# A hybrid encoder step: the exponentials of the prompt heads are turned undivided, and six bits of a search stand between row maxima

## The chip, the core and the metric

The kernel runs on one core of one Trainium2 chip. The metric is the time of one execution in device microseconds. A core has five engines that work side by side and wait for one another by semaphores: TensorE (PE, matmuls; PEld is its weight load), VectorE (DVE), ScalarE (ACT), GpSimd (POOL) and SyncE (SP, which issues DMAs). Each engine works through its own instructions strictly in the order in which the code issues them; a wait stops everything behind it on that engine.

## The reference

One step of a trunk with two layers, on a prompt of 512 tokens and on 8 samples of 16 new tokens with 1024 cached ones. Layer 0 mixes the tokens by sparse attention: an indexer scores the keys, each query keeps its best k, and softmax attention with 8 heads runs over them. Cut to that part (the rest, a gated MLP in layer 1, a convolutional feed-forward and a gated addition in both, is not touched by the change):

```python
s = einsum('bqhd,bkd->bqhk', qi, ki) * (IDX_DIM ** -0.5)
score = einsum('bqhk,bqh->bqk', relu(s), wi * (N_IDX_HEADS ** -0.5))
score = where(admissible, score, NEG_INF)
_, idx = lax.top_k(score, k_sel)          # 128 for the prompt, 256 for a sample
logits = einsum('bqgrd,bqkgd->bqgrk', qg, kg) * (HEAD_DIM ** -0.5)
p = softmax(where(valid, logits, NEG_INF), axis=-1)
o = einsum('bqgrk,bqkgd->bqgrd', p, vg)   # then o @ w_out
```

## The kernel before, in words

All 640 token columns (512 of the prompt, 128 of the samples) go through together, in tiles of 128. Every product with weights is done in three float32r passes (high x high, high x low, low x high), so ScalarE splits off the high part of each block of weights and VectorE the low part. Nothing is scheduled by a tool: the order on each engine is the order of the Python code of that engine's block, and the semaphores are written out by hand.

The selection masks the keys instead of gathering them. For the samples, the 256th largest score of each of 128 rows (8 samples x 16 tokens) is found by a search over its bits from 30 down to 0. One bit (`search`) is three VectorE instructions: a comparison of the 1040 scores with a guess, which also counts, and two on a single column that set the next guess. The table `BITS` says how many bits are done during which tile of the projections (tiles 4 to 8: 5, 6, 6, 6 and 8). `hide_samples` makes of the last guess the mask `bias_s`, with a scan that settles ties. For the prompt, rounds of `find` (the 8 largest of a row) and `mark` (strike them out) select the keys; the rounds left over stand between the row maxima of the samples and of the stage p1.

Attention is a list `att` of 40 heads, numbered s: 0 to 7 are the heads of the first prompt tile (stage p0, 128 keys), 8 to 15 the samples (all 8 heads of a sample are one entry, 1040 keys), 16 to 23, 24 to 31 and 32 to 39 the heads of prompt tiles 1 to 3 (p1, p2 and p3, with 256, 384 and 512 keys). All engines first wait in `after_projection`. Then each runs its own loop over s:

- TensorE, in turn s: `turn_probs(s-1)` transposes the probabilities into PSUM, `weigh(s-2)` multiplies them with the values, `turn_rows(s-3)` (for samples alone) turns the result, `scores(s+1)` makes mask plus logits of the next head.
- VectorE: `row_max(s)` takes the reciprocal of the sum of head s-1, then the negated maximum of head s.
- ScalarE, in turn s: `normalise(s-1)` divides the exponentials of a prompt head, then comes the exponential of s with its sum, `turn_out_probs(s-1)` (the transposed probabilities out of PSUM), `take_turned(s-3)` for samples, `take_out(s-2)` (the result out of PSUM).

For a prompt head the probabilities are divided before they are transposed, and the weighting has the values as the stationary operand, so its result comes out turned already. For a sample the raw exponentials are transposed, the result is divided as it leaves PSUM (into `o_row`), turned by TensorE, and copied into `qT`.

Before turn NA-3 (s = 37), the first block of the output projection's weights is split: `split_hi` on ScalarE, `split_lo` on VectorE. Behind the last head ScalarE casts the results (`a_hi`, L986), VectorE subtracts (`a_lo`, L1297), and the output projection starts (L638).

## Time and profile before

| | |
|---|---|
| median of 3 runs | 1687.17 us (1685.6 to 1688.04) |
| profiled execution, its own time | 1686.9 us |
| its span | 1685.0 us |
| TensorE busy | 1615.4 us (96%), 11098 matmuls |
| VectorE busy | 928.8 us (55%) |
| ScalarE busy | 629.7 us (37%) |
| mean granted TensorE clock | 0.985 of full |
| chain that ended last | PE 87%, DVE 7%, ACT 3%, issue 2% |

The span goes from the first to the last instruction in the trace; the time of an execution is a little longer. A busy share is a mean over stages that have different limits, and matmuls are pipelined with modelled ends, so a busy TensorE need not be one at its peak. The chain is followed back from the last instruction, at each step to what released it.

### The profile page before, as it was taken

The page shows a single profiled execution, that of the slowest core. Times are in us where ns is not written, and L with a number is a line of the kernel's source. Part 1 is how long each engine was busy: PE and PEld are TensorE (multiplying, and loading weights), DVE is VectorE, ACT ScalarE, POOL GpSimd, SP SyncE. Part 2 cuts the span into 40 slices and gives each one's busy share as a digit, 9 for nine tenths or more (in the row PEclk, how much of TensorE's full clock was granted, in tenths as well). Part 3 has the DMA queues.
Part 4 walks back from the last instruction along what each step waited for, and adds up shares of the span by engine and source line. Part 5 has one row for each costly group of instructions (what it writes and reads, how often), then busy time and mean ns, then how long its engine had stood idle before and what let it go on. Part 6 is the DMA issues. An engine that isn't in the chain of part 4 may idle for free.

```text
span 1685.0 us, 25745 instructions
## 1 busy us (share of the span) xinstructions
PE 1615.4 (96%) x11098; PEld 1544.5 (92%) x11106; DVE 928.8 (55%) x1287; ACT 629.7 (37%) x928; POOL 172.1 (10%) x270
## 2 busy tenths in 40 slices
PE   7999778889999999999999999999999999999998
PEld 7759745589999999999999999999999999999998
DVE  5279966344665256525665715527663466346653
ACT  4546444744332133213354524325331233123441
POOL 2000000002110011001121201022110011001200
PEclk9999889999999999999999999999999999999999
DMA  5212445021122212221132221321222122211321
GB/s 216 80 50 76 161 167 200 1 76 68 59 76 101 74 53 76 95 71 61 67 110 84 88 85 52 115 75 51 75 76 101 51 75 75 100 51 63 113 92 47
DMA packets 27938, 143.50 MB, mean 85 GB/s; under 512 B 3393, under 2 KB 7105, under 8 KB 14641
## 3 DMA queue, kind: packets, MB, share of 16 engines
q1 hardware_dynamic: 26912, 139.03, 23.5%
q0 software_dynamic: 768, 2.81, 0.5%
q8 instruction: 87, 1.43, 0.4%
q14 instruction: 27, 0.21, 0.0%
q10 hardware_dynamic: 144, 0.02, 0.0%
HBM read 136.29 MB, written 5.43 MB: 84 GB/s over the span
## 4 chain that ended last, share of the span: by engine, by line
PE 87%; DVE 7%; ACT 3%; issue 2%; DMA 0%; SPq 0%; DVEq 0%; ACTq 0%
PE psum L638 71%; PE psum L684 5%; DVE bias_s L1202 2%; PE psum L724 2%; PE psum L552 1%; PE psum L491 1%; PE psum L500 1%; PE psum L594 1%; DVE stat L1248 1%; PE psum L673 1%; PE psum L539 1%; DVE w_lo L1291 1%; PE psum L587 1%; PE psum L511 1%; PE psum L569 1%
## 5 line engine op out<-in xcount | busy, mean ns | idle before, releaser
L638 PE MATMUL psum<-a_hi,w_hi 128*128 128x384 f32 (+2 forms) x1920 | 439.2, 310 | 7.5 <-DVE a_lo L1297 7.5
L638 PE MATMUL psum<-a_lo,w_hi 128*128 128x384 f32 (+2 forms) x1920 | 437.8, 309 | 0.0
L638 PE MATMUL psum<-a_hi,w_lo 128*128 128x384 f32 (+2 forms) x1920 | 437.7, 309 | 0.0
L638 PEld LDWEIGHTS psum<-a_hi,w_hi 128*128 128x128 f32 x1920 | 341.7, 188 | 9.7 <-issue 6.7
L638 PEld LDWEIGHTS psum<-a_hi,w_lo 128*128 128x128 f32 x1920 | 342.3, 188 | 0.0
L638 PEld LDWEIGHTS psum<-a_lo,w_hi 128*128 128x128 f32 x1920 | 342.2, 188 | 0.0
L1291 DVE TENSOR_TENSOR w_lo<-w_raw,w_hi 128x2048 fp32r<-128x2048 f32 (+1 forms) x101 | 227.2, 2250 | 120.7 <-ACT w_hi L983 120.6
L983 ACT ACTIVATE w_hi<-w_raw 128x2048 fp32r<-128x2048 f32 (+1 forms) x102 | 189.6, 1859 | 172.1 <-PE psum L638 172.1
L638 PE MATMUL psum<-g_hi,w_hi 128*128 128x320 f32 x832 | 191.0, 311 | 2.4 <-DVE u_act L1503 1.6
L1139 ACT ACTIVATE conv<-conv_in,convw 128x656 f32<-128x656 f32 x88 | 82.4, 937 | 293.5 <-DVE conv_in L1537 293.5
L638 PE MATMUL psum<-g_hi,w_lo 128*128 128x320 f32 x832 | 189.9, 310 | 0.0
L638 PE MATMUL psum<-g_lo,w_hi 128*128 128x320 f32 x832 | 189.9, 310 | 0.0
L1474 DVE TENSOR_TENSOR xT<-psum,xT 128x640 f32<-128x640 f32 x64 | 52.7, 823 | 197.7 <-PE psum L638 197.3
L1536 DVE TENSOR_TENSOR conv_in<-psum,inv_rms 128x512 f32<-128x512 f32 x88 | 60.6, 688 | 153.4 <-PE psum L638 153.3
L638 PEld LDWEIGHTS psum<-g_hi,w_hi 128*128 128x128 f32 x832 | 139.4, 189 | 4.0 <-issue 2.2
L638 PEld LDWEIGHTS psum<-g_hi,w_lo 128*128 128x128 f32 x832 | 139.7, 189 | 0.0
L638 PEld LDWEIGHTS psum<-g_lo,w_hi 128*128 128x128 f32 x832 | 139.7, 189 | 0.0
L1597 POOL COPY tails<-conv_in 128x18 f32<-128x18 f32 x88 | 44.1, 501 | 661.3 <-DVE conv_in L1537 661.3
L684 PE MATMUL psum<-w_hi,a_hi 128*128 128x256 f32 x288 | 83.1, 289 | 0.0
L684 PE MATMUL psum<-w_lo,a_hi 128*128 128x256 f32 x288 | 82.4, 286 | 0.0
L684 PE MATMUL psum<-w_hi,a_lo 128*128 128x256 f32 x288 | 82.3, 286 | 0.0
L1544 DVE SCALAR_TENSOR_TENSOR conv<-conv_in,convw,conv 128x656 f32<-128x656 f32 x88 | 79.4, 902 | 3.1
(228 smaller groups left out, 1944.1 us busy)
## 6 DMA issues: line engine op xcount, KB each, us to landing
w_raw<-in_weights SPq DMA_DIRECT2D x93, 1024.0 KB, 4.8
key_b<-in_keyT SPq DMA_DIRECT2D x8, 1024.0 KB, 7.9
val_b<-in_val SPq DMA_DIRECT2D x8, 1024.0 KB, 4.8
w_raw<-in_weights SPq DMA_DIRECT2D x8, 768.0 KB, 4.1
kidx_b<-in_kidxT SPq DMA_DIRECT2D x8, 512.0 KB, 3.5
xT<-in_xT SPq DMA_DIRECT2D x2, 1280.0 KB, 6.8
out_yT<-xT SPq DMA_DIRECT2D x8, 320.0 KB, 2.2
xT<-in_xT SPq DMA_DIRECT2D x3, 640.0 KB, 8.4
```

The costliest lines, as they stand in the source:

```text
L491: pe.matmul(psum[:, c, 0:w], qi_blk[:, b, :], kidx_b[b % 2][:, k0:k0 + w], start=True, stop=True).then_inc(idx_ready, 1)
L638: last = pe.matmul(psum[:, 2 * j + bank, 0:t1 - t0], w[:, k, P * j:P * j + P], x[:, k, t0:t1], start=(k == 0 and n == 0), stop=(k == K - 1 ...
L684: last = pe.matmul(out, x[:, k, P * t:P * t + P], ww[:, k, :], start=(k == 0 and n == 0), stop=(k == KC - 1 and n == 2))
L724: last = pe.matmul(psum[:, 2 * (c % 2) + i, 0:T // 2], w[:, k, P * c:P * c + P], x[:, k, i * T // 2:(i + 1) * T // 2], start=(k == 0 and n ...
L983: act.activation(w_hi(u)[:, 0:n], w_raw[u % 2][:, 0:n], ACT.Copy).then_inc(w_hi_ready, 1)
L1139: act.activation(co[j][:, :], ci[j][:, 2:2 + CW], ACT.Identity, bias=convw[:, l, ch, 3:4], scale=convw[:, l, ch, 2:3])\
L1202: dve.tensor_scalar(bias_s[:, :], score_s[:, :], f32(guess[:, 0:1]), 0.0, ALU.is_ge, ALU.add, accum_out=found[:, 1:2]).then_inc(counted, 1)
L1291: dve.tensor_tensor(w_lo(u)[:, 0:n], w_raw[u % 2][:, 0:n], f32(w_hi(u)[:, 0:n]), ALU.subtract)\
L1474: dve.tensor_tensor(xn, bank2(j, T // 2), xn, ALU.add).then_inc(free_dve, 1)
L1536: dve.tensor_tensor(halves(ci[j][:, 2:2 + TP]), bank2(j, 256), halves(inv_rms[:, 0:TP]), ALU.mult)
L1544: dve.scalar_tensor_tensor(out=co[j][:, :], in0=ci[j][:, 0:CW], scalar=convw[:, l, ch, 0:1], in1=co[j][:, :], op0=ALU.mult, op1=ALU.add).t ...
L1597: ins = pool.tensor_copy(tails[:, j * FC + c, :].rearrange("p (i e) -> p i e", e=2), padded(conv_in[c % 2][j], NB + 1))
```

## The change

Two parts. First, the exponentials of a prompt head are no longer divided on ScalarE (`normalise` and its semaphore are gone): TensorE transposes them raw, the weighting takes them as the stationary operand and the values as the moving one, and then prompt heads go the way of the samples: `take_out` scales by the inverse sum into `o_row`, `turn_rows` turns that on TensorE, `take_turned` copies it into `qT`. Second, tile 8 of the projections holds two bits of the search in place of eight; the last six stand one each between the row maxima 0 to 6 of p0, and `hide_samples` comes behind them in one piece, with row maximum 7 after it.

```diff
--- before.py
+++ after.py
@@ -49,7 +49,8 @@
 TOPK_P, TOPK_S = 128, 256
 KV = 3
 WIDE_ROUNDS = 10
-BITS = {4: 5, 5: 6, 6: 6, 7: 6, 8: 8}
+BITS = {4: 5, 5: 6, 6: 6, 7: 6, 8: 2}
+LATE_BITS = 6
 ZQ, ZK, ZV, ZQI, ZKI, ZW, ZEND = 0, 1024, 1280, 1536, 2048, 2112, 2120
 PADW = 2 + TP + NB * (2 + TQ) + 16
 CW = TP + NB * (2 + TQ)
@@ -306,19 +307,17 @@
         att += [("p", j, h) for j in range(1, 4) for h in range(H)]
         NA = len(att)
         S0, S1 = H, H + NB
-        att_p = [s for s in range(NA) if att[s][0] == "p"]
         bias_ready, n_bias_ready = sem("bias_ready"), counts(["p0", "s", "p1", "p2", "p3"])
         logits, n_logits = sem("logits"), counts(range(NA))
         neg_max, n_neg_max = sem("neg_max"), counts(range(NA))
         exp_done, n_exp_done = sem("exp_done"), counts(range(NA))
         sum_inverse, n_sum_inverse = sem("sum_inverse"), counts(range(NA))
-        prob_ready, n_prob_ready = sem("prob_ready"), counts(att_p)
         pt_ready, n_pt_ready = sem("pt_ready"), counts(range(NA))
         pt_taken, n_pt_taken = sem("pt_taken"), counts(range(NA))
         out_ready, n_out_ready = sem("out_ready"), counts(range(NA))
         out_taken, n_out_taken = sem("out_taken"), counts(range(NA))
-        o_scaled, n_o_scaled = sem("o_scaled"), counts(range(S0, S1))
-        o_turned, n_o_turned = sem("o_turned"), counts(range(S0, S1))
+        o_scaled, n_o_scaled = sem("o_scaled"), counts(range(NA))
+        o_turned, n_o_turned = sem("o_turned"), counts(range(NA))
         s_key = [sem(f"s_key{i}") for i in range(KV)]
         s_val = [sem(f"s_val{i}") for i in range(KV)]
         key_new, n_key_new = sem("key_new"), counts(range(NB))
@@ -556,10 +555,7 @@
 
             def turn_probs(s):
                 kind, a, h = att[s]
-                if kind == "p":
-                    pe.wait_ge(prob_ready, n_prob_ready[s])
-                else:
-                    pe.wait_ge(exp_done, n_exp_done[s])
+                pe.wait_ge(exp_done, n_exp_done[s])
                 if kind == "p":
                     if S1 <= s < S1 + 3:
                         pe.wait_ge(pt_taken, n_pt_taken[S1 - 1])
@@ -584,8 +580,8 @@
                 o = psum[:, 6 + s % 2, :]
                 if kind == "p":
                     for i in range(a + 1):
-                        last = pe.matmul(o[:, 0:P], vtok[:, i, P * (h // R):P * (h // R) + P],
-                                         probsT[s % 2][:, i, :], start=(i == 0), stop=(i == a))
+                        last = pe.matmul(o[:, 0:P], probsT[s % 2][:, i, :],
+                                         vtok[:, i, P * (h // R):P * (h // R) + P], start=(i == 0), stop=(i == a))
                 else:
                     pe.wait_ge(s_val[a % KV], 32 * (a // KV + 1))
                     for i in range(9):
@@ -606,7 +602,7 @@
                     turn_probs(s - 1)
                 if 2 <= s < NA + 2:
                     weigh(s - 2)
-                if S0 <= s - 3 < S1:
+                if s >= 3:
                     turn_rows(s - 3)
                 if s + 1 < NA:
                     scores(s + 1)
@@ -881,30 +877,21 @@
                 kind, a, h = att[s]
                 act.wait_ge(out_ready, n_out_ready[s])
                 o = psum[:, 6 + s % 2, 0:P]
+                act.wait_ge(sum_inverse, n_sum_inverse[s])
+                act.activation(o_row[s % 2][:, :], o, ACT.Copy, scale=stat[:, 3, s:s + 1]).then_inc(o_scaled, 1)
+
+            def take_turned(s):
+
+                kind, a, h = att[s]
+                act.wait_ge(o_turned, n_o_turned[s])
+                o = psum[:, 6 + s % 2, P:2 * P]
                 if kind == "p":
                     act.activation(qT[:, h, P * a:P * a + P], o, ACT.Copy).then_inc(out_taken, 1)
                 else:
-                    act.wait_ge(sum_inverse, n_sum_inverse[s])
-                    act.activation(o_row[s % 2][:, :], o, ACT.Copy, scale=stat[:, 3, s:s + 1]).then_inc(o_scaled, 1)
-
-            def take_turned(s):
-
-                kind, a, h = att[s]
-                act.wait_ge(o_turned, n_o_turned[s])
-                act.activation(qT[:, :, TP + TQ * a:TP + TQ * a + TQ],
-                               psum[:, 6 + s % 2, P:2 * P].rearrange("p (h q) -> p h q", q=TQ), ACT.Copy)\
-                   .then_inc(out_taken, 1)
-
-            def normalise(s):
-
-                kind, a, h = att[s]
-                pr = probs[s % 2][:, 0:P * (a + 1) if kind == "p" else KEYS]
-                act.wait_ge(sum_inverse, n_sum_inverse[s])
-                act.activation(pr, pr, ACT.Copy, scale=stat[:, 3, s:s + 1]).then_inc(prob_ready, 1)
+                    act.activation(qT[:, :, TP + TQ * a:TP + TQ * a + TQ], o.rearrange("p (h q) -> p h q", q=TQ), ACT.Copy)\
+                       .then_inc(out_taken, 1)
 
             for s in range(NA + 3):
-                if s - 1 in n_prob_ready:
-                    normalise(s - 1)
                 if s < NA:
                     kind, a, h = att[s]
                     w = P * (a + 1) if kind == "p" else KEYS
@@ -918,7 +905,7 @@
                     split_hi(FIRST["attn_out"])
                 if 1 <= s <= NA:
                     turn_out_probs(s - 1)
-                if S0 <= s - 3 < S1:
+                if s >= 3:
                     take_turned(s - 3)
                 if 2 <= s < NA + 2:
                     take_out(s - 2)
@@ -1217,15 +1204,11 @@
                 dve.tensor_scalar(found_eq[:, :], score_s[:, :], last, None, ALU.is_equal)
                 link(dve.tensor_scalar(bias_s[:, :], score_s[:, :], last, 0.0, ALU.is_gt, ALU.add,
                                        accum_out=found[:, 2:3]))
-                row_max(1)
                 dve.tensor_tensor_scan(found_rank[:, :], found_eq[:, :], found_eq[:, :], 0.0, ALU.add, ALU.bypass)
                 link(dve.tensor_scalar(found[:, 3:4], found[:, 2:3], -1.0, float(TOPK_S), ALU.mult, ALU.add))
-                row_max(2)
                 link(dve.scalar_tensor_tensor(out=found_eq[:, :], in0=found_rank[:, :], scalar=found[:, 3:4],
                                               in1=found_eq[:, :], op0=ALU.is_le, op1=ALU.mult))
-                row_max(3)
                 link(dve.tensor_tensor(found_eq[:, :], found_eq[:, :], bias_s[:, :], ALU.add))
-                row_max(4)
                 dve.tensor_scalar(bias_s[:, :], found_eq[:, :], 0.5, NEG, ALU.is_lt, ALU.mult).then_inc(bias_ready, 1)
 
             def hide(j):
@@ -1251,8 +1234,11 @@
             link(dve.memset(bias_p[0][:, :], 0.0))
             dve.memset(bias_p[0][0:64, 64:P], NEG).then_inc(bias_ready, 1)
             row_max(0)
+            for bit in range(LATE_BITS - 1, -1, -1):
+                search(dve, link, [bit])
+                row_max(LATE_BITS - bit)
             hide_samples()
-            for s in range(5, S0):
+            for s in range(LATE_BITS + 1, S0):
                 row_max(s)
             for s in range(S0, S1):
                 row_max(s)
```

On VectorE, at the start of attention, before: the last bits of the search, the first mask of p0, row maximum 0, and then `hide_samples` with the next row maxima in it.

```order
L1202 TENSOR_SCALAR bias_s,found<-score_s,guess 128x1040 [waits dve_chain]
L1205 TENSOR_SCALAR guess<-found 128x1 [waits counted]
L1210 TENSOR_TENSOR guess<-guess 128x1 [waits dve_chain]
L1251 MEMSET bias_p0 128x64 [waits turned_out,s_kout,free_act,dve_chain]
L1252 MEMSET bias_p0 64x64 [waits dve_chain]
L1248 TENSOR_REDUCE stat<-psum 128x1 [waits logits]
L1217 TENSOR_SCALAR found_eq<-score_s,guess 128x1040
L1218 TENSOR_SCALAR bias_s,found<-score_s,guess 128x1040
L1239 RECIPROCAL stat<-stat 128x1 [waits exp_done,dve_chain]
L1248 TENSOR_REDUCE stat<-psum 128x1 [waits logits]
L1221 SCALAR_TENSOR_TENSOR found_rank<-found_eq 128x1040
```

In the changed kernel the first mask stands behind the second bit of tile 8, and bits follow on row maxima.

```order
L1189 TENSOR_SCALAR bias_s,found<-score_s,guess 128x1040 [waits dve_chain]
L1192 TENSOR_SCALAR guess<-found 128x1 [waits counted]
L1194 SCALAR_TENSOR_TENSOR guess<-guess 128x1 [waits dve_chain]
L1234 MEMSET bias_p0 128x64 [waits turned_out,s_kout,free_act,dve_chain]
L1235 MEMSET bias_p0 64x64 [waits dve_chain]
L1231 TENSOR_REDUCE stat<-psum 128x1 [waits logits]
L1189 TENSOR_SCALAR bias_s,found<-score_s,guess 128x1040
L1192 TENSOR_SCALAR guess<-found 128x1 [waits counted]
L1194 SCALAR_TENSOR_TENSOR guess<-guess 128x1 [waits dve_chain]
L1222 RECIPROCAL stat<-stat 128x1 [waits exp_done,dve_chain]
L1231 TENSOR_REDUCE stat<-psum 128x1 [waits logits]
L1189 TENSOR_SCALAR bias_s,found<-score_s,guess 128x1040
```

The six bits moved behind the first mask and row maximum 0; the reciprocals and maxima stay one each per head.

On TensorE, one turn of stage p2, before: transposes, weighting, mask, logits (`probs0` and `probs1` are the two buffers of the exponentials).

```order
L569 MATMUL psum<-ident,probs0 128x128 [waits pt_taken,prob_ready]
L569 MATMUL psum<-ident,probs0 128x128 x2
L587 MATMUL psum<-probsT1,vtok 128x128 [waits out_taken,pt_taken]
L587 MATMUL psum<-probsT1,vtok 128x128 x2
L538 MATMUL psum<-bias_p2,ident_b 128x384 [waits exp_done]
L539 MATMUL psum<-kT,qT 128x384
```

The same turn in the changed kernel.

```order
L565 MATMUL psum<-ident,probs0 128x128 [waits pt_taken,exp_done]
L565 MATMUL psum<-ident,probs0 128x128 x2
L583 MATMUL psum<-vtok,probsT1 128x128 [waits out_taken,pt_taken]
L583 MATMUL psum<-vtok,probsT1 128x128 x2
L597 MATMUL psum<-ident,o_row0 128x128 [waits o_scaled]
L537 MATMUL psum<-bias_p2,ident_b 128x384 [waits exp_done]
L538 MATMUL psum<-kT,qT 128x384
```

The transposes wait for the exponential itself, the two operands of the weighting have changed sides, and one transpose of `o_row` stands ahead of the mask and the logits of the next head.

On ScalarE, one turn of p2 and the start of the next, before.

```order
L915 ACTIVATE probs1,stat<-psum,stat 128x384 [waits pt_ready,neg_max]
L874 ACTIVATE probsT0<-psum 128x384 [waits out_ready,pt_ready]
L885 ACTIVATE qT<-psum 128x128 [waits out_ready]
L903 ACTIVATE probs1<-probs1,stat 128x384 [waits sum_inverse]
L915 ACTIVATE probs0,stat<-psum,stat 128x384 [waits pt_ready,neg_max]
```

The same in the changed kernel.

```order
L902 ACTIVATE probs1,stat<-psum,stat 128x384 [waits pt_ready,neg_max]
L870 ACTIVATE probsT0<-psum 128x384 [waits out_ready,pt_ready]
L889 ACTIVATE qT<-psum 128x128 [waits o_turned]
L881 ACTIVATE o_row1<-psum,stat 128x128 [waits sum_inverse,out_ready]
L902 ACTIVATE probs0,stat<-psum,stat 128x384 [waits pt_ready,neg_max]
```

The 384 columns wide division is gone, and of the two instructions of 128 columns one waits for the turned row and one for the inverse sum.

## Rows read from the trace of the kernel before

**Rows 1.** The page's chain that ended last: shares of the span by line.
```profile
PE psum L638 71%; PE psum L684 5%; DVE bias_s L1202 2%; PE psum L724 2%; PE psum L552 1%; PE psum L491 1%; PE psum L500 1%; PE psum L594 1%; DVE stat L1248 1%; PE psum L673 1%; PE psum L539 1%; DVE w_lo L1291 1%; PE psum L587 1%; PE psum L511 1%; PE psum L569 1%
```

**Rows 2.** Timeline, VectorE, p0: start, length, engine, line, out<-in, count [idle before<-releaser].
```profile
201.81 1.29 DVE L1202 TENSOR_SCALAR_CACHE_REDUCE bias_s<-score_s,guess 128x1040 bf16<-128x1040 f32 x1
...
203.53 1.30 DVE L1202 TENSOR_SCALAR_CACHE_REDUCE bias_s<-score_s,guess 128x1040 bf16<-128x1040 f32 x1
...
205.29 0.11 DVE L1251 MEMSET bias_p<- 128x64 uint32 x1
...
206.78 0.75 DVE L1217 TENSOR_SCALAR found_eq<-score_s,guess 128x1040 f32<-128x1040 f32 x1
...
213.71 0.29 DVE L1248 TENSOR_REDUCE stat<-psum 128x1 f32<-128x128 f32 x1 [0.48 <-PE psum L539]
...
216.16 0.16 DVE L1239 RECIPROCAL stat<-stat 128x1 f32<-128x1 f32 x1
...
220.54 0.29 DVE L1248 TENSOR_REDUCE stat<-psum 128x1 f32<-128x128 f32 x1 [0.58 <-PE psum L539]
```

**Rows 3.** Timeline, ScalarE and the sync queue (SPq), end of the projections.
```profile
195.97 1.30 ACT L1090 ACTIVATE kT<-psum 128x640 f32<-128x640 f32 x2
...
197.33 0.69 SPq L436 DMA_DIRECT2D key_b<-in_keyT  x1
```

**Rows 4.** Groups by line, 197 to 350: count | busy us, mean ns | idle before<-releasers.
```profile
L903 ACT ACTIVATE probs<-probs,stat 128x128 f32<-128x128 f32 (+3 forms) x32 | 17.9, 560 | 4.9 <-DVE stat L1239 4.7
...
L569 PE MATMUL psum<-ident,probs 128*128 128x128 f32 x80 | 16.7, 307 | 16.2 <-ACT probs L903 15.8
```

**Rows 5.** Stretches: us, busy PE, PEld, DVE, ACT, POOL, PE clock, DMA share, GB/s.
```profile
197.00:206.00 9.00, 0.27 (x2) 0.30 (x3) 7.95 (x22) 0.26 (x1) 0.98 (x4) 0.59 0.94 347
...
222.00:224.00 2.00, 2.00 (x9) 0.50 (x9) 0.00 (x0) 0.02 (x1) 0.00 (x0) 0.88 0.00 0
...
335.00:340.00 5.00, 1.86 (x11) 0.99 (x9) 2.73 (x3) 3.22 (x6) 0.00 (x0) 1.00 0.00 0
```

**Rows 6.** Timeline, TensorE, score matmuls of samples 0 and 4.
```profile
223.51 1.08 PE L552 MATMUL psum<-key_b,q_smp 128*64 128x512 f32 x4
...
251.30 1.98 PE L552 MATMUL psum<-key_b,q_smp 128*64 128x512 f32 x4
```

**Rows 7.** Timeline, TensorE, in p1 (first row) and p2.
```profile
287.53 0.44 PE L569 MATMUL psum<-ident,probs 128*128 128x128 f32 x2 [0.48 <-ACT probs L903]
...
314.03 0.55 PE L569 MATMUL psum<-ident,probs 128*128 128x128 f32 x3 [0.32 <-ACT probs L903]
314.41 0.83 PE L587 MATMUL psum<-probsT,vtok 128*128 128x128 f32 x6
...
315.24 0.81 PE L539 MATMUL psum<-kT,qT 128*128 128x384 f32 x2
316.12 0.55 PE L569 MATMUL psum<-ident,probs 128*128 128x128 f32 x3
```

**Rows 8.** Timeline, VectorE, p1 to p3: row maxima, and the split of weights.
```profile
293.08 0.42 DVE L1248 TENSOR_REDUCE stat<-psum 128x1 f32<-128x256 f32 x1
...
295.14 0.42 DVE L1248 TENSOR_REDUCE stat<-psum 128x1 f32<-128x256 f32 x1
...
301.23 0.42 DVE L1248 TENSOR_REDUCE stat<-psum 128x1 f32<-128x256 f32 x1 [0.79 <-PE psum L539]
...
303.14 0.56 DVE L1248 TENSOR_REDUCE stat<-psum 128x1 f32<-128x384 f32 x1 [0.69 <-PE psum L539]
...
320.78 0.69 DVE L1248 TENSOR_REDUCE stat<-psum 128x1 f32<-128x512 f32 x1 [1.14 <-PE psum L539]
...
333.94 0.69 DVE L1248 TENSOR_REDUCE stat<-psum 128x1 f32<-128x512 f32 x1 [0.82 <-PE psum L539]
337.27 2.29 DVE L1291 TENSOR_TENSOR w_lo<-w_raw,w_hi 128x2048 fp32r<-128x2048 f32 x1 [2.64 <-ACT w_hi L983]
```

**Rows 9.** Timeline, ScalarE, the cast of the output projection's operand.
```profile
348.77 5.13 ACT L986 ACTIVATE a_hi<-qT 128x640 fp32r<-128x640 f32 x8
```

## The prediction

> **What bounds the kernel now.** I read the chain of waits on the page first: 71% of the span is one line, the TensorE products of L638, and the search bits (DVE, L1202), the sample scores (L552) and the row maxima (L1248) hold 1 to 2% each [rows 1]. So the products outside attention cannot move by this change; what can move lies between the end of the projections (about 197 us) and the first product of the output projection (350 us). I then read the timelines of the engines in this stretch, one stage at a time, and asked in each which wait ends last.
>
> Stage p0 (heads 0 to 7) cannot begin before the VectorE has done eight search bits: it writes the first mask at 205.29 [rows 2], though the last projected tile is there at 197.27 and the sync queue, which waits for the same three semaphores, goes on at 197.33 [rows 3]. The samples follow; they wait for one another's exponentials and for their keys. In p1 (heads 16 to 23) the VectorE sets the pace, with a round of find and mark per head (2.06 us from one row maximum to the next). In p2 and p3 it is TensorE together with the division on ScalarE: TensorE stood idle 15.8 us in all before its transposes, released by L903 [rows 4].
>
> **Part one: six bits moved into p0.** A bit takes 1.72 us (201.81 to 203.53) [rows 2]. Eight of them back from 205.29 begin near 191.5; two would be done by 195, so the VectorE then starts p0 with the sync queue at 197.33. From the first mask to the end of the first row maximum it took 205.29 to 206.78, 1.49, so row maximum 0 is done at 198.8. Then come six rounds of a bit and a row maximum. The maximum costs some 0.3 (0.29 by its row, the reciprocal before it overlaps), so 2.02 a round, 12.1 together; I add 0.25 because the first reciprocal waits for the first exponential and its table load. TensorE and ScalarE have 2 us for each head there and took 1.71 before (four heads from 213.71 to 220.54), so they don't hold the VectorE up: 211.2. Hiding the samples took 206.78 to 216.16, with four row maxima and a wait of 0.48 inside: 9.38 - 4 x 0.3 - 0.48 = 7.7, now in one piece, and row maximum 7 is behind it. It starts near 219.0, before at 220.54 [rows 2]: 1.5 earlier. The VectorE thus starts 8 us earlier, carries 10.3 us more, and loses its idle gaps.
>
> What is late next is TensorE's clock. In the second half of p0 it had work close together, and the granted clock came back in 222:224 (0.88 of full), just as sample 0 began. In the change TensorE has nothing from about 213 to 219.5, while the samples are hidden. After its idle stretch in 197:206 the clock had fallen (0.59 in the mean) [rows 5]. A group of four score matmuls took 1.98 us at half clock and 1.08 at full [rows 6]; sample 0 has two and its masks, so all at half clock it costs up to 1.8 more than at full, and part of it was at half before. Ends: 1.5 saved, the clock as before; or 0.3 lost, sample 0 all at half. I take half of the way: **-0.7**.
>
> The Trainium skill (TensorE: Matmul & The Clock Gate, section "HAM oscillation") says that a gap between bursts of matmuls can put the array back to half rate, so that the next burst starts cold. By that rule this part would be +0.3 and the whole sum -4.1. The trace agrees in 197:206, but not everywhere: in 335:340 TensorE was busy 1.86 of 5.00 us and kept 1.00 [rows 5]; by that row it is -1.5 and the sum -5.9.
>
> The samples themselves keep their order. Three more turned rows (heads 5 to 7) fall into their first steps, where TensorE waits for an exponential anyway; without that cover they cost 0.13 each.
>
> **Part two: the division leaves the path.** Removed: 32 divisions of the exponentials on ScalarE, 0.56 each in the mean [rows 4], and the wait of the transposes for them, which also held a VectorE reciprocal. Added per prompt head: one TensorE transpose and a ScalarE copy from PSUM. Three transposes hold TensorE 0.38 (314.03 to 314.41) [rows 7], so one is 0.13. The copy that goes out of PSUM was there already; now there are two small ones for one small and one wide. The new waits: the turned row stands in TensorE's queue ahead of the next head's scores and waits for the scaled row; ScalarE's copy of it stands ahead of the next scaled row. Both look back one whole head, so in a head of 2 us they are met early. The operands of the weighting change sides, at the same 128x128.
>
> - p1. The pace of find and mark stays (293.08 to 295.14) [rows 8]. What goes is the waits ahead of it and behind it. TensorE waited 0.48 for the division of head 16 [rows 7], and as long for that of 17; without the first, the scores of head 18 are 0.6 earlier, and VectorE runs its rounds 0.6 earlier. Behind the last round VectorE waited 0.79 for head 23's scores (301.23), and head 24's came at 303.14 [rows 8]; both chains lose a division with its handover, about 1.0 together. Ends: nothing (VectorE alone bounds), -2.2. I take **-1.6**.
> - p2. Now 303.14 to 320.78 for eight heads, 2.205 each [rows 8]. TensorE's own work is at most 2.09 (transposes at 314.03 and 316.12); the second start came just after a division's end, so there is a wait in it. It begins the weighting 0.17 before the modelled end of the transposes; if it can do so behind the product at 315.24 (0.81), its own work is 1.85 [rows 7]. With 0.13 for the turned row: 1.98 to 2.22. I take 2.05, as TensorE stood idle in every second head: 8 x 0.155 = **-1.2** (ends -1.8 and +0.1).
> - p3. Five intervals from 320.78 to 333.94, 2.63 each [rows 8]; transposes, weighting and product grow with the width, and the same reasoning leaves 0.08 a head: **-0.4** (ends -1.0 and +0.5).
> - Tail. The split of the next weights (2.29 on VectorE at 337.27) [rows 8] stays, between heads 37 and 38, and the first operand is cast at 348.77 [rows 9]. From the split's end (339.56) that is 9.2 us with two divisions of 512 columns on the path; each costs its time, a reciprocal and two handovers, about 1.0. Against that the last head has a turned row and one more copy behind it, 0.8. Ends 0 and -2; I take **-1.2**.
>
> Sum: -0.7 - 1.6 - 1.2 - 0.4 - 1.2 = -5.1. From there on TensorE has work without a gap, so the shift reaches the end whole. The profiled execution had a span of 1685.0 in a time of 1686.9; it gives 1681.8. It lay 0.3 under the median of the runs, 1687.17, which gives 1682.1. I forecast 1682.0 us, 0.3% faster.
>
> **Rivals.**
> First: TensorE is already the bound in p2 and p3, so that each added transpose is paid there. For it: 2.09 of own work in 2.205 [rows 7, 8]. Against it: the 15.8 us idle before the transposes. Then p2 and p3 lose 16 x 0.13 - 0.1 = 2.0 in place of gaining 1.6: -5.1 + 3.6 = -1.5, 1685.7.
> Second: the clock takes p0's gain and falls again in the tail, where TensorE has shorter bursts; the output projection would then start at half clock for some us, like the sample that took 1.98 for 1.08 [rows 6], about 2 us lost. For it: the fall after 197. Against it: 335:340 at 1.00 [rows 5]. -5.1 + 1.0 + 2 = -2.1, 1685.1.
> Third, slower: the way of the result closes a ring: weighting, scaled row, turned row, copy, and the weighting two heads on waits for the copy. If it is longer than two heads, TensorE stands at the turned row as long as it stood at the division, and the 24 later heads pay 0.13 and, say, one more handover of 0.1: +5.5, with the tail's 0.8 and no gain in p0: +6.3, 1693.5. It decides only if scaled row, turn and copy with their handovers, some 1.3 us, take over 3; I see no row for that.
> Fourth: the moved bits do nothing, since VectorE is the engine that p0 waits for in both: part one 0, 1682.8. That is within the forecast's range.
>
> **How the numbers follow.** Forecast with the fourth 0.72, first 0.12, second 0.11, third 0.05. A difference of 0.2%, 3.4 us, is about what a measurement here tells from none; 1683.8 is the border. The forecast's cases go from -8 (1679; all the lower ends would be -8.5) to -3 (1684), with a tenth of them beyond the border. So faster 0.72 x 0.9 + 0.23 x 0.3 = 0.72, slower 0.05 and a little of the others, 0.06, the same 0.22. The range goes from 1678.6 to 1685.9, which takes in the first two rivals' values.
>
> **What would show it.** In the profile after: the first row maximum near 198.5 and the last of p0 near 219; a clock of 0.5 at the start of sample 0; no wait of the transposes for a division; p2 at 2.05 a head; the operand cast near 343.7. I am wrong if TensorE waits for the scaled rows, if p2 stays at 2.2, or if the samples take longer than before between row maximum 7 and the first of p1.

## The result, and the profile after

The changed kernel takes 1679.66 us (median, 1676.94 to 1680.47), the kernel before, beside it on the same chip, 1687.61; the ratio is 0.9946, 95% interval 0.993 to 0.9962. The ratio makes 1678.1 of the median that I started from, 1687.17; I forecast 1682.0 with 1678.6 as the lower end. So the change gains 7.5 us by its median, 8.0 beside the runs of the same chip and 9.1 by the ratio, where I said 5.1. The profiled execution, at 1676.94, is the fastest of four: span 1675.0, 10.0 below that of before. The chain that ended last is now 92% TensorE, 3% VectorE and 2% ScalarE.

The p0 stage in the timeline of VectorE after (start, length, line, operation, [idle before <- releaser]): the first mask, row maxima 0, 7 and 8.

```profile
197.35 0.11 DVE L1234 MEMSET bias_p<- 128x64 uint32 x1 [2.61 <-ACT kT L1077]
...
198.32 0.29 DVE L1231 TENSOR_REDUCE stat<-psum 128x1 f32<-128x128 f32 x1 [0.68 <-PE psum L538]
...
218.76 0.27 DVE L1231 TENSOR_REDUCE stat<-psum 128x1 f32<-128x128 f32 x1
224.04 1.24 DVE L1231 TENSOR_REDUCE stat<-psum 128x1 f32<-128x1040 f32 x1 [4.32 <-PE psum L551]
```

Row maximum 7 is 1.78 earlier than in [rows 2] (I said 1.5), but that of sample 0 only 0.94 earlier. TensorE shows why, at the samples' start:

```profile
219.58 0.61 PE L548 MATMUL psum<-bias_s,onehot 128*128 128x512 bf16 x1 [6.49 <-ACT probs L902]
220.12 1.98 PE L551 MATMUL psum<-key_b,q_smp 128*64 128x512 f32 x4
```

It idled 6.49 us behind head 6, and the first score group takes 1.98: half clock. Before, the same group took 1.34; the 1.08 at 223.51 in [rows 6] is the second group, which takes 1.09 now.

```profile
221.91 1.34 PE L552 MATMUL psum<-key_b,q_smp 128*64 128x512 f32 x4 [0.49 <-ACT probsT L874]
```

The granted clock was at half long ahead of the pause, and in both kernels: 0.50 in every slice of 4 us from 206 to 222. So the pause didn't bring it down. Before, it came back within this first group; now sample 0 starts 1.8 us earlier, and it comes back behind it.

The p2 stage on TensorE, one head from the transposes to the next head's, answers to [rows 7]:

```profile
304.76 0.49 PE L565 MATMUL psum<-ident,probs 128*128 128x128 f32 x3
305.09 0.83 PE L583 MATMUL psum<-vtok,probsT 128*128 128x128 f32 x6
305.76 0.27 PE L597 MATMUL psum<-ident,o_row 128*128 128x128 f32 x1
305.87 0.33 PE L537 MATMUL psum<-bias_p,ident_b 128*128 128x384 bf16 x1
306.03 0.81 PE L538 MATMUL psum<-kT,qT 128*128 128x384 f32 x2
306.67 0.49 PE L565 MATMUL psum<-ident,probs 128*128 128x128 f32 x3
```

No row has a wait, and each begins before the modelled end of the one ahead. From start to start: transposes 0.33, weighting 0.67, turned row 0.11, bias 0.16, scores 0.64, together 1.91. The lines from 197 to 340 us (count | busy, mean ns | idle before <- releasers) answer to [rows 4]:

```profile
L565 PE MATMUL psum<-ident,probs 128*128 128x128 f32 x80 | 15.4, 291 | 4.1 <-ACT probs L902 3.9
...
L597 PE MATMUL psum<-ident,o_row 128*128 128x128 f32 x40 | 12.2, 304 | 0.6 <-ACT o_row L881 0.6
```

The idle time before the transposes has gone from 16.2 to 4.1 us, and the turned rows wait 0.6 in all, for 40 of them: the ring of the third rival is nowhere closed.

The table holds the stretches of every profile, from start to start of row maxima (by the timeline of VectorE; s is the index of the attention step) and, for the tail, to the cast of the output operand. "Mark" is the start of an earlier, unchanged split of weights, ahead of attention; the column behind it is the way from there to sample 0.

| kernel | mark | mark to s=8 | samples 8-16 | p1 16-24 | p2 24-32 | p3 32-37 | tail | cast at |
|---|---|---|---|---|---|---|---|---|
| before | 127.63 | 97.35 | 58.06 | 20.10 | 17.64 | 13.16 | 14.83 | 348.77 |
| after | 127.47 | 96.57 | 55.39 | 18.21 | 15.24 | 12.01 | 13.84 | 338.73 |
| after_again | 127.70 | 96.56 | 56.10 | 19.84 | 15.24 | 12.01 | 13.84 | 341.29 |
| bits_only | 126.17 | 98.27 | 57.40 | 21.71 | 17.67 | 13.16 | 17.17 | 351.55 |
| raw_only | 127.92 | 94.57 | 58.56 | 19.83 | 15.24 | 12.01 | 13.84 | 341.97 |
| turn_twice | 126.27 | 97.59 | 57.79 | 19.94 | 16.00 | 12.56 | 14.26 | 344.41 |
| spread_bits | 126.31 | 95.73 | 56.69 | 19.82 | 15.24 | 12.01 | 13.83 | 339.63 |
| bit3 | 127.84 | 96.06 | 57.10 | 19.83 | 15.24 | 12.01 | 13.84 | 341.92 |
| before_keys | 125.19 | 98.50 | 51.77 | 20.10 | 17.64 | 13.16 | 17.17 | 343.53 |
| raw_keys | 126.45 | 95.36 | 52.08 | 18.21 | 15.24 | 12.01 | 13.83 | 333.18 |
| keys_first | 125.12 | 97.50 | 52.13 | 18.21 | 15.24 | 12.01 | 13.84 | 334.05 |
| spread_keys | 125.13 | 95.36 | 51.06 | 19.19 | 15.24 | 12.01 | 13.83 | 331.82 |

From the cast to the end it is 1335.5 to 1338.0 us in all twelve (1336.2 before, 1336.3 after), so between these two the table holds the whole difference. p2, p3 and the tail are the same to 0.01 in all kernels with part two, except the one that doubles the turned row. p1 has two levels, 18.21 and 19.82 to 19.94 with part two (19.19 once), 20.10 and 21.71 without; the longer one goes with a granted clock of 0.59 to 0.99 in 278:286, the shorter with 1.00. The samples and the way to them vary. The way from the mark to sample 0 also hangs on where the mark lies: before and before_keys have the same code up to there and 97.35 and 98.50, after and keys_first 96.57 and 97.50, raw_only and raw_keys 94.57 and 95.36; the earlier mark has the longer way each time.

### The profile page after: what moved, and what is told of

It is laid out like the page before. It is cut to its first block, busy times and chain, and to the rows that moved or that the text cites. A ratio compares the mean times of both kernels' runs of the same rounds, so it can differ in the third digit from the quotient of the medians.

```text
span 1675.0 us, 25851 instructions
## 1 busy us (share of the span) xinstructions
PE 1617.9 (97%) x11138; PEld 1548.9 (92%) x11138; DVE 927.9 (55%) x1287; ACT 621.4 (37%) x928; POOL 168.1 (10%) x270
## 4 chain that ended last, share of the span: by engine, by line
PE 92%; DVE 3%; ACT 2%; issue 1%; DMA 0%; SPq 0%; ACTq 0%; DVEq 0%
PE psum L634 71%; PE psum L680 9%; PE psum L720 2%; PE psum L551 1%; PE psum L490 1%; PE psum L583 1%; PE psum L499 1%; PE psum L590 1%; PE psum L538 1%; PE psum L669 1%; PE psum L510 1%; PE psum L565 1%; ACT a_hi L973 1%; DMA xT<-in_xT 0%; PE psum L759 0%
```

## Experiments

Each median stands beside the median of before on the same chip: 1688.11 for the first four kernels, 1687.27 for the next four, 1687.68 for the last two.

**after_again.** The changed kernel once more, no edit.

> The changed kernel once more. Of the 10.0 us between the two profiled spans, 2.7 lie between row maximum 8 and row maximum 16, in the samples, which neither part of the change touches. Theory A: these 2.7 are TensorE's clock, which fell to half inside two samples of the profiled execution before and in none after, and that differs from one execution to the next; then a profile taken here can show half clock in a sample again, the samples are then as long as before, and the times lie some 7 to 9 us under the kernel before, spread over 3 us. Theory B: the change itself shortens the samples; then the samples are again 55.4 us from row maximum 8 to 16, and the clock stays full in them.

1680.4 us (1679.87 to 1682.82), ratio 0.9953 [0.9937, 0.997]. The granted clock fell to 0.72 and 0.86 in 262:266 and 266:270, and to 0.85 and 0.72 in 278:286, where the first profile had 1.00 throughout: p1 took 1.63 longer than in the first profile, the samples 0.71. That is theory A, though the samples are not as long as before (56.10 for 58.06). So the first profile is a lucky one: 10.0 is not what the change is worth in most executions.

**bits_only.** Part one without part two: the kernel before with the bits moved, divisions on the exponentials as they were.
```
-BITS = {4: 5, 5: 6, 6: 6, 7: 6, 8: 8}
+BITS = {4: 5, 5: 6, 6: 6, 7: 6, 8: 2}
+LATE_BITS = 6
...
+            for bit in range(LATE_BITS - 1, -1, -1):
+                search(dve, link, [bit])
+                row_max(LATE_BITS - bit)
             hide_samples()
```

> Part one alone: six bits between the row maxima of p0, the division stays. Theory A (the parts add up): sample 0's row maximum comes 0.9 us earlier than before, as in the changed kernel, the stages p1 to p3 keep the paces of before (2.2 us in p2, 2.6 in p3), and the time is about 1 us under before, 0.5 to 1.5. Rival: the bits need the short way of the raw exponentials, because TensorE and ScalarE with the division take longer per head than a bit and a row maximum (1.98 us); then row maximum 7 comes at or after 220.5 and the time is the same as before or up to 2 us longer.

1688.84 us, ratio 1.0003 [0.9991, 1.0015]: nothing, so the parts don't add up as theory A has it. The rival gave the right time for a reason that doesn't hold: row maximum 7 is not late (217.86, 91.69 behind the mark for 92.91 before). What it gains is lost between it and row maximum 8, 6.58 for 4.44: sample 0 runs at half clock (its two score groups take 1.98 and 1.91). Its profile also has a clock fall in the tail, after the split of the weights (TensorE there, same columns as above):

```profile
340.88 1.11 PE L570 MATMUL psum<-ident,probs 128*128 128x128 f32 x4 [3.59 <-ACT probs L904]
341.79 1.91 PE L588 MATMUL psum<-probsT,vtok 128*128 128x128 f32 x8
```

In the kernel before, the same place reads

```profile
340.44 0.66 PE L569 MATMUL psum<-ident,probs 128*128 128x128 f32 x4 [3.59 <-ACT probs L903]
...
340.94 1.06 PE L587 MATMUL psum<-probsT,vtok 128*128 128x128 f32 x8
```

The wait for the division is the same 3.59, yet the eight weighting products take 1.91 for 1.06, and the tail 17.17 for 14.83.

**raw_only.** Part two without part one.
```
-BITS = {4: 5, 5: 6, 6: 6, 7: 6, 8: 2}     # and LATE_BITS = 6 between the row maxima
+BITS = {4: 5, 5: 6, 6: 6, 7: 6, 8: 8}     # row maxima 1 to 4 inside the samples' mask, as before
```

> Part two alone: raw exponentials are turned and the sum divides the result; all eight bits in tile 8, the samples hidden between row maxima as before. Theory A: p1 to the cast of the output projection's operand gains what the profile of the changed kernel shows there, 1.9 + 2.4 + 1.2 + 1.0 = 6.5 us, p0 up to 1 more, since its last heads have no division either; the time is 6.5 to 7.5 us under before. Rival: half of the gain is the early start and its changed clock, so that this one is only 4 us or less under before.

1676.74 us (1675.43 to 1680.33), ratio 0.9931 [0.9914, 0.9948]: the whole gain, if not more (its interval overlaps those of the changed kernel). It is also more than theory A said, 11.4 by the median and 8.8 at the least by the interval: p0 gives 2.8 (97.35 to 94.57), not up to 1. Row maximum 7 is as early as with part one (218.53), and TensorE reaches sample 0 in work and at full clock:

```profile
218.91 0.27 PE L596 MATMUL psum<-ident,o_row 128*128 128x128 f32 x1
219.69 1.08 PE L550 MATMUL psum<-key_b,q_smp 128*64 128x512 f32 x4 [0.50 <-ACT probsT L869]
```

From the mark to sample 0 it is 94.57, 2.0 less than with both parts.

**turn_twice.** The changed kernel with every prompt head's row turned a second time.
```
+                    pe.transpose(psum[:, 6 + s % 2, P:2 * P], o_row[s % 2][:, :], ident[:, :])
```

> The changed kernel with every prompt head's result turned twice by TensorE (the second transposes the same row into the same place). Theory A: in p2 and p3 TensorE's own work is the pace (1.91 and 2.40 us), so each head of these 16 pays one more transpose, 0.11: p2 at 2.02, p3 at 2.51, 1.8 us in all and 0.2 in the tail, while p1, paced by VectorE at 1.91, pays nothing; 2 us over the changed kernel. Rival: the chain of maximum, exponential, copies and their handovers is the pace; then the second transpose hides and the time is that of the changed kernel within 0.5 us.

1683.4 us (1680.55 to 1685.52), ratio 0.9966 [0.9953, 0.9978]. p2 goes from 1.905 to 2.00 a head and p3 from 2.40 to 2.51: one turned row's 0.11 is paid (almost) whole in both. In p2 and p3 TensorE's own work is the pace now; in p1 it is not (19.94 beside 19.84 in after_again, both with the fall of the clock). The median is 3.0 over after_again where 2 was expected; p2, p3 and the tail of the profile hold 1.7 of it.

**spread_bits.** VectorE's work of the first tile dealt out differently.
```
-            for bit in range(LATE_BITS - 1, -1, -1):     # one bit, one row maximum; then the mask in one piece
+            for s in range(1, 4):                         # two bits, one row maximum;
+                search(dve, link, [2 * (3 - s) + 1])      # row maxima 4 to 7 between the mask's operations
+                search(dve, link, [2 * (3 - s)])
+                row_max(s)
```

> The changed kernel with the same VectorE work in the first tile, dealt out differently: two search bits ahead of each of row maxima 1 to 3, and row maxima 4 to 7 between the operations that make the samples' mask, so that no block of the mask's operations stands ahead of row maximum 7. Theory (part one's gain of row maximum 7 is given back because TensorE idles 6.49 us while VectorE makes the mask in one piece, and comes to sample 0 at half clock): row maximum 7 stays near 218.8 or comes a little earlier, the longest pause of TensorE in that stretch falls below 3 us, the granted clock at 218 to 222 is 1.00, row maximum 8 comes at 222.5 to 223.0 instead of 224.0, and the time is 1 to 1.5 us below the changed kernel. Rival (the order of VectorE's work is of no account, the samples wait for their mask in any case): row maximum 8 stays at 223.8 to 224.3 and the time within 0.5 us.

1678.17 us, ratio 0.9952 [0.9935, 0.9969]: 1.5 under the changed kernel by the medians, level with it by the ratios (0.9946 and 0.9953), so the times don't show the gain; mark to sample 0 is 95.73, 0.84 less than after. The pause of TensorE is 0.81 as the theory says, but the clock is not back:

```profile
217.85 1.98 PE L551 MATMUL psum<-key_b,q_smp 128*64 128x512 f32 x4 [0.81 <-ACT probsT L870]
```

So what the profile gains comes from row maximum 7 (216.35; 1.25 nearer to the mark than after's, since VectorE makes the mask no longer in one block), and the half clock doesn't need the long pause: it was 0.50 from 202 to 218, 0.64 in 218:222. That part of the theory fell. In raw_only TensorE was busy 3.90 of 4.00 us in 214:218, the clock rose there (0.74), and 218:222 had 1.00.

**raw_keys** and **keys_first.** SyncE's queue, with part two alone and with the whole change.
```
+            for b in range(NB):
+                if b <= KV:
+                    load_keys(b)
+                if KV <= b < NB - 1:
+                    load_keys(b + 1)
+                load_values(b)
```

`load_keys` and `load_values` hold the lines that stood in this loop; there, the keys of a sample stood behind the wait of the values of the sample ahead of it.

> Part two alone, with one more edit: SyncE issues the keys of sample b+1 ahead of the values of sample b, whose issue waits for a buffer of the values; before, the keys stood behind that wait. Theory (TensorE's waits ahead of a sample's scores, 1.62, 0.40, 1.04 and 1.14 us in the changed kernel's profile, are for keys that were issued late, and the stretches of half clock in the samples follow such waits): these waits fall below 0.3 us each, the samples take 53 us or less from row maximum 8 to 16 (55.4 in the changed kernel's profile, 56.3 and 58.6 in other profiles at a half clock in part of it), with granted clock 1.00 throughout; the time is 3 to 5 us below part two alone (1676.7), and the runs spread less. Rival (the transfers themselves are the limit, or the values wait in the keys' place): the wait moves to the values or the next keys, the samples take 55 us or more, and the time is within 1 us of part two alone.

> The changed kernel with the same edit of SyncE's order as raw_keys (keys of sample b+1 ahead of the values of sample b). Theory: as there, the waits for keys go and the samples take 53 us or less; the time is 3 to 5 us below the changed kernel (1679.7), and it stays 2 to 4 us above raw_keys, since part one adds a cold sample 0 and nothing more. Rival one (transfers are the limit): within 1 us of the changed kernel. Rival two (part one does help where the samples no longer wait): the time is equal to raw_keys or below it.

1671.37 us (1670.93 to 1673.14), ratio 0.9904 [0.9888, 0.9919], and 1671.66 (1670.81 to 1673.64), 0.9905 [0.9889, 0.9921]. The changed kernel waited before its sample scores for keys (one of four such rows; "issue" says that the profile names no releaser, and that it is the keys is shown by the edit):

```profile
247.16 0.38 PE L548 MATMUL psum<-bias_s,onehot 128*128 128x512 bf16 x1 [1.62 <-issue]
```

All four are gone from both, the samples take 52.1 and the clock is 1.00 in all of 234:286; the same stretch of raw_only (us, busy PE, PEld, DVE, ACT, POOL, PE clock, DMA share, GB/s) had

```profile
262.00:266.00 4.00, 2.35 (x7) 0.50 (x10) 1.29 (x6) 0.28 (x2) 0.00 (x0) 0.74 0.85 299
...
278.00:286.00 8.00, 5.89 (x51) 4.86 (x52) 3.99 (x14) 2.41 (x8) 0.00 (x0) 0.79 0.58 237
```

and keys_first

```profile
262.00:266.00 4.00, 3.85 (x49) 2.82 (x48) 3.90 (x11) 2.81 (x6) 0.00 (x0) 1.00 0.20 78
...
278.00:286.00 8.00, 7.77 (x71) 5.99 (x72) 6.05 (x18) 4.43 (x17) 0.00 (x0) 1.00 0.00 0
```

The gains, 5.4 and 8.0 by the medians and 4.6 and 6.9 by the ratios, are near or over the upper end of the expected 3 to 5. The two are equal in time, and not 2 to 4 apart as the theory said; by the mark column keys_first loses 2.14 at sample 0, but its profile had 1.33 in hand at the mark, and an earlier mark has the longer way.

**bit3.** Three bits early and five late.
```
-LATE_BITS = 6
+LATE_BITS = 5      # and one bit more in the earlier place
```

> The changed kernel with one search bit moved back: three bits at the earlier place instead of two, five between the row maxima. VectorE idles 2.61 us ahead of row maximum 0 in the changed kernel's profile, and one bit takes about 2.0 us. Theory (the bits fill an idle stretch as long as there is one; only bits beyond it are worth moving): row maximum 0 stays within 0.3 us of 198.3, row maximum 7 comes 1.5 to 2.0 us earlier (216.8 to 217.3), and if TensorE still idles over 5 us ahead of the samples, sample 0 is still cold and keeps 0.5 to 0.9 of that from being given on; the time is 0.7 to 2 us below the changed kernel. Rival (the samples' mask or the keys set sample 0, not row maximum 7): row maximum 8 and the time stay within 0.4 us.

1677.41 us (1677.09 to 1680.26), ratio 0.9937 [0.9922, 0.9952]. Row maximum 0 came at 198.69, 7 at 217.71 (1.05 earlier, 1.42 counted from the mark, for 1.5 to 2.0 expected); from the mark to sample 0, 96.06, 0.51 gained. The median is 2.2 below after's, more than the profile explains, which is of the slowest of the five runs: in direction as the theory says, inconclusive in size.

**before_keys.** The same edit of SyncE's queue on the kernel before.

> The kernel before with SyncE's order alone changed (keys of sample b+1 issued ahead of the values of sample b), none of the change under study. Question: does the change itself gain anything in the samples (55.4 us from row maximum 8 to 16 in the changed kernel's profile, 58.1 before), or was that difference the waits for keys and the clock that falls after them. Theory (waits and clock): the samples take 52.0 to 52.6 us here too, as in raw_keys (52.1) and keys_first (52.1); the time is 1680 to 1682, that is 6 to 8 us below the kernel before, and the distance to keys_first is then 8.5 to 10 us, the sum of p0, p1, p2, p3 and the tail without the samples. Rival (the earlier row maximum 7 or the changed division speeds up the samples): the samples take 54.5 us or more, and the time stays within 4 us of before.

1682.05 us (1678.66 to 1684.22), ratio 0.9968 [0.9955, 0.9982]. The samples take 51.77, as with the change: the change itself has nothing to give there, and what the profiles after show is the waits for keys and the clock behind them. keys_first is 10.4 below this kernel, a little over what was expected (8.5 to 10); 2.34 of the profiles' difference is a fall of the clock in the tail, as in bits_only, and 1.5 lies behind the cast.

**spread_keys.** Both remedies.

> Both remedies together: the changed kernel with VectorE's work of the first tile dealt out as in spread_bits (row maximum 7 at 216.35, TensorE's pause ahead of sample 0 at 0.81 us) and SyncE's order as in keys_first. Theory (spread_bits gained 2 us at row maximum 8 against the changed kernel, keys_first 1.4 us there by bringing kT's cast forward; the two overlap in part): row maximum 8 at 220.5 to 221.5, the samples 52.1 us, and the time 0.5 to 2 us below keys_first (1671.66), at 1669.7 to 1671.2, the best version so far. Rival (sample 0 waits for something else once row maximum 7 is early, such as the samples' mask or the cold clock): row maximum 8 at 222 or later, and the time within 0.5 us of keys_first.

1669.26 us (1668.56 to 1671.27), ratio 0.9897 [0.9884, 0.991]: the best version, some 18 us below the kernel before and 10 below the changed one. Below keys_first it is 2.4 by the medians, but the ratios don't tell the two apart. Sample 0 came at 220.49 and the samples took 51.06, both at or below what was expected. The 1.4 us that the expectation gives to keys_first at row maximum 8 are no effect of its edit that a run shows: they were there at the mark already (125.12 for 127.47), ahead of the edit. Its profile still has a fall of the clock (0.57 in 270:274), which p1 pays with 0.98.

## Why the prediction was off

- **Direction and mechanism: right.** Part two takes the division off the path; the whole gain is its own (raw_only 1676.74, bits_only ratio 1.0003). Part two was tried as one piece: no run takes the division away without turning the rows.
- **p2, the step that failed.** I took 2.05 for a head, between 1.98 (own work 1.85, and 0.13 for the turned row) and 2.22 (own work 2.09) [rows 7]. Start to start it is 1.91 with the turned row, below the lower end of 1.98 that I allowed, and turn_twice shows that nothing else holds the pace. About half of the error is that I leaned away from 1.98: the 2.09 did hold a wait, and it goes whole. The other half is the own work. The three transposes take 0.33 and not 0.38 when they follow without a pause (both transpose rows of p2 in [rows 7] begin behind the end of the row ahead), and the turned row 0.11 and not 0.13. The exchange of the operands costs nothing: the weighting takes 0.67 from start to start in both kernels. The term is -2.4 for the -1.2 that I took.
- **p3.** The same error: 2.40 a head for 2.55, -1.15 for -0.4. Together p2 and p3 miss 1.95 of the 2.4 to 4.0 by which I fell short.
- **p1: right in size, in part by errors that cancel.** With the clock up it is -1.9 for -1.6, and with the fall in 278:286 the same (21.71 to 19.84). Ahead of the rounds it gives 0.70 for 0.6 and behind them 0.70 for 1.0. But the pace of find and mark, which I held fixed, went from 2.04 to 1.91 in the mean of four rounds, 0.5 in all; why, no run shows.
- **Tail: right in size** where the clock of before stayed up, -1.0 for -1.2. But behind the division's wait of 3.59 the clock fell in two of three profiles without part two, which cost 2.34 more up to the cast, and up to the cast in none of nine with it. So the change takes away a risk there that I had put on its own side, in the second rival.
- **Part one: right for the profile, -0.8 from mark to sample 0 for -0.7, but by the wrong split, so by luck.** It is part two that brings row maximum 7 forward in p0, which I had left at nothing: alone it shortens this way by 2.8 (97.35 to 94.57). Part one on top of it gives 2.0 back (94.57 to 96.57; with the keys early 95.36 to 97.50, of which the earlier mark may be a part). Alone it shows neither gain nor loss: 98.27 is 0.9 over before and 0.2 under before_keys. In times this loss is not resolved: 3.7 between raw_only and after_again with intervals that overlap, 0.3 between raw_keys and keys_first.
- **Samples: 0 forecast, -2.67 in the profile.** Not the change's (before_keys, after_again). It comes and goes with the clock, by execution.
- **The four terms at equal clock** (p1 -1.89, p2 -2.40, p3 -1.15, tail -0.99) make -6.4; with the -0.8 up to sample 0 it is -7.2. That lies within the intervals of both measurements of the changed kernel (6.4 to 11.8 and 5.1 to 10.6 under before). The times say -7.5 to -9.1; for the rest there is the clock in the samples, p1 and the tail, and no run here separates them.
- **Rivals.** The first (TensorE already bound in p2) was wrong of before, and true of after, as the 0.11 of turn_twice shows. The second was right about the start of the output projection and its price. The clock is at 0.50 within 2 us of its first product in all profiles with part two but the first, and in two of three without. Counted from the cast, the second split of weights behind it comes 2.69 later in after_again (363.59 - 341.29) than in after (358.34 - 338.73), where the clock stayed up. By the end only 0.3 of this is left (1336.6 for 1336.3), because in after and before the clock falls further on, where after_again keeps 1.00: in after to 0.91 in 398.73:418.73, and to 0.98 and 0.93 in the two slices of 20 us from 998.73. So the equal ways from the cast to the end don't say that a fall costs nothing. The same split in after and in after_again, in VectorE's timelines:

```profile
358.34 2.29 DVE L1277 TENSOR_TENSOR w_lo<-w_raw,w_hi 128x2048 fp32r<-128x2048 f32 x1 [2.61 <-ACT w_hi L970]
```

```profile
363.59 2.29 DVE L1277 TENSOR_TENSOR w_lo<-w_raw,w_hi 128x2048 fp32r<-128x2048 f32 x1 [2.61 <-ACT w_hi L970]
```

- **The other rivals.** The slower third is excluded by the 0.6 of waiting above. The fourth, that the moved bits do nothing, is the one that bits_only bears out.
- **The rule of the Trainium skill** (TensorE: Matmul & The Clock Gate, section "HAM oscillation"), that a gap sends the next burst off cold, is borne out only in part. Sample 0 of the changed kernel is no case of it, since the clock was at half before the 6.49 of idling; the same holds for spread_bits, where the half rate was there with a pause of 0.81. In the tail it held in two profiles and not in a third, 3.59 idle in all of them.

## What to carry to other kernels

Take what an engine can do in a loop from start to start of neighbouring rows without a wait between them, and with no pause ahead of the first: three transposes held TensorE 0.38 behind a pause and 0.33 without one. Where an own work and a wait can't be told apart, ask which rows of the loop begin behind the end of the one ahead, before taking the middle. Before a change is credited with a stretch, see whether the same stretch repeats in a second profile of the same kernel: p2 and p3 repeated to 0.01, the samples moved by several us. And look at what stands in a queue behind a wait: the kernels with one load reordered are 5.4 to 8.0 us faster here, nearly as much as the whole change gained.

## What was not expected of the hardware

The same instructions with the same idle time in front ran at either clock in different executions: 1.06 or 1.91 us behind 3.59 of waiting. Behind 2.16 to 2.17 us of waiting for the cast, the clock was at half within 2 us in ten of twelve profiles; the two that kept it, before and after, fell later. The mark, ahead of all the edits, lay between 125.12 and 127.92; in 20:40 us the granted clock was 0.83 where it was late (127.47 and more), 0.91 where it lay between and 1.00 where it was early (125.2 and less). It was 1.00 in the profiles of keys_first, before_keys and spread_keys and 0.91 in that of raw_keys, which has the same edit; whether their edit, which is much later in the program, has to do with it, or only chance, is left open. Part of the 5.4 to 8.0 us of the key loads may be this and not the samples.
